# Group 1's weights split in the first pair of each attention, and the third pair reordered, in a hybrid attention and linear recurrence layer

## The chip, the cores and the metric

The kernel runs on one core of one Trainium2 chip. The metric is the device time of one execution in microseconds. A core has five engines with their own instruction streams: TensorE (PE), VectorE (DVE), ScalarE (ACT), GpSimd (POOL) and SyncE (SP), which here issues all DMAs. They wait for each other by semaphores. SBUF is the working memory, PSUM (eight banks) takes what PE writes.

## What is computed

One decoder layer on x of 2048 rows by 1024: RMS norm with shift and scale from a conditioning vector, one input projection to (attention q, k, v, gate; recurrence q, f, i, gate), a sliding-window attention with 16 query heads and 4 key heads of 64 columns, a gated linear recurrence with 8 heads of 128, and one output projection with gate and residual. All is float32. What bears on the change is the attention:

```
aq = rope(rms_norm(aq.reshape(B, S, 16, 64), q_norm_w), positions)
ak = rope(rms_norm(ak.reshape(B, S, 4, 64), k_norm_w), positions)
attn = sliding_window_attention(aq, ak, av, sinks) * silu(ag)
# blocks of 128 rows; each block of queries sees its own and the previous block of keys
s = q k^T * hd ** -0.5 ; s = where(mask, s, -inf)
m = max(max(s), sink) ; p = exp(s - m)
denom = sum(p) + exp(sink - m) ; o = (p / denom) v
```

## The kernel before

The 2048 rows are done as two segments of 1024 (s = 0, 1). For each segment there is a matrix product part (three units, `gemm_unit`), then the attention, then the recurrence. The output projection comes last. Each product is made of three single-pass products of split operands: a "hi" part (a copy rounded to the fast type, made by ACT) and a "lo" part (the rest, made by DVE as raw minus hi), so each weight has to be split before PE can use it.

**The attention** of a segment goes through 4 groups of heads with 8 blocks of 128 rows, 32 blocks b, taken in 16 pairs m (`att_pair`, one function for PE, one for ACT, one for DVE, each with an order written out by hand; POOL has `att_iter` for each block). In pair m PE projects the blocks 2m and 2m+1 (`project_block`, 24 matmuls of 384 columns each), turns q and k of the blocks j = 2m-2 and j+1 (`turn_qk`), turns the probabilities of the blocks p = 2m-4 and p+1 (`turn_p`), multiplies them with v (`values`) and makes new scores (`scores`) for the blocks j and j+1. So the third pair, m = 2, is the first with probabilities in it.

The path of a block b: PE projects it; ACT squares it (`squares_and_v`); DVE sums the squares (`sum_squares`); POOL makes the variance and the inverse root (L2739, L2741, `inverse_root`); DVE scales (`norm_qk`); POOL rotates q and k (L2779 to L2795; for block 0 DVE does q in `rotate_first`); PE turns them; ACT copies the hi (`turned_hi`), DVE the lo (`turned_lo`); PE makes scores; DVE masks them and takes the maxima (`mask_scores`); ACT exponentiates (`exps`); DVE inverts the sums (`invert_den`); ACT scales (`normalise`); PE turns (`turn_p`); ACT and DVE copy half of it each (`p_copy`). `project_block(b)` waits until block b-2 has been scaled, as both use one bank (`qkv_free`).

**The weights** of a group g (1536 KB) go to one buffer, `raw[0]`, and are split in 4 parts: `att_weights_hi` on ACT (semaphore `hi_ok`) and `att_weights_lo` on DVE (`lo_ok`). `next_weights(s, m)` on ACT and DVE says which parts of the next group are split in which pair. For group 1 in before: ACT makes parts 0 and 1 at the end of pair 1, 2 and 3 at the end of pair 2; DVE makes 0 and 1 in the middle of pair 2, 2 and 3 in the middle of pair 3. SP loads the next group once the last one has been split (`load_next`); group 1's load comes after the gate blocks of the attention, group 0's is asked for in the last unit of the products.

**Between products and attention** ACT, DVE, POOL and SP meet (`meet`, `phase_end`): none goes on until all five engines have arrived. SP arrives when all stores of the products have landed. PE arrives and goes on without waiting. Just ahead of it ACT makes the sines (`rotary_angles`) and DVE the rotary tables.

Of the kernel before, what the change touches and what calls it, by code (L numbers as in the profile page):

```python
# [29 lines left out]
QB = QUAD // P  # L30
# [46 lines left out]
def hybrid_layer(nc, x, xT, cT, pos, norm_w, w_ada, b_cols, b_gate, w_in, qk_w, sinks, rec_w, lbT, w_out,  # L77
                 ident_d, masks_d, causal_d, freq_d, out, mixed_T, nat, gate_T, x_T_d, root_d, a21_d, carry_k, carry_v):
    with ExitStack() as ctx:
# [421 lines left out]
        def _(sp):  # L501
# [60 lines left out]
            def gemm_unit(s, u):  # L562
# [33 lines left out]
                if not last:  # L596
                    sp.wait_ge(wlo_ok, PRODS * n + 7)
                    load_quarter(n + 1, B21)
                for c in range(4):
                    sp.wait_ge(comb_ok, comb(n, COMB_21, c))  # L600
                    block_out(s, u, u3[c], nat_u3, 1, 0, c)
# [21 lines left out]
            def attention(s):  # L623
# [40 lines left out]
                load_next(0)  # L664
# [228 lines left out]
        def _(pe):  # L893
# [335 lines left out]
            def att_pair(s, m):  # L1229

                j, p = 2 * m - 2, 2 * m - 4
                if 2 <= m <= PAIRS:
                    turn_qk(s, j)
                if m < PAIRS:
                    project_block(s, 2 * m, range(KH))
                    if m == 1:
                        turn_qk(s, j)
                    project_block(s, 2 * m, range(KH, KT))
                    project_block(s, 2 * m + 1, range(KH))
                    if m >= 1:  # L1240
                        turn_qk(s, j + 1)
                    project_block(s, 2 * m + 1, range(KH, KT - 2))
                    if m >= 2:
                        turn_p(s, p)
                    project_block(s, 2 * m + 1, range(KT - 2, KT))
                    if m >= 2:
                        turn_p(s, p + 1)
# [227 lines left out]
        def _(act):  # L1475
# [137 lines left out]
            def rotary_angles(s):  # L1613
                act.wait_ge(trig_step, s * 10 + 10)
                act.activation(sinv[:], ang[:], ACT.Sin).then_inc(trig_a, 1)
                act.activation(turns[:], ang[:], ACT.Abs).then_inc(trig_a, 1)
                act.wait_ge(trig_a, s * 3 + 2)
                act.activation(cosv[:], turns[:], ACT.Sin, bias=half_pi[:, 0:1], scale=-1.0).then_inc(trig_a, 1)

# [79 lines left out]
            def next_weights(s, m):  # L1699

                g, at = m // (NBLK // 2), m % (NBLK // 2)
                if g + 1 < GROUPS:
                    for part in (() if g == 0 else (0,), (0, 1) if g == 0 else (1,), (2, 3), ())[at]:
                        act.wait_ge(raw_in[0], 16 * w_use(s, 0, g + 1) + 16)
                        att_weights_hi(g + 1, part)
                elif at < 2:
                    rec_weights_hi(s, 0, (at,))

            def att_pair(s, m):

                j, p = 2 * m - 2, 2 * m - 4
                if 1 <= m <= PAIRS:
                    turned_hi(s, j)
                if 2 <= m <= PAIRS:
                    exps(s, p)
# [231 lines left out]
        def _(dve):  # L1947
# [412 lines left out]
            def next_weights(s, m):  # L2360

                g, at = m // (NBLK // 2), m % (NBLK // 2)
                if g + 1 < GROUPS:
                    for part in ((), () if g == 0 else (0,), (0, 1) if g == 0 else (1,), (2, 3))[at]:
                        att_weights_lo(s, g + 1, part)
                elif 1 <= at <= 2:
                    rec_weights_lo(s, 0, (at - 1,))

            def att_pair(s, m):

                j, p = 2 * m - 2, 2 * m - 4
                if 2 <= m <= PAIRS:
                    mask_scores(s, p)
                if 1 <= m <= PAIRS:
                    norm_qk(s, 2 * m - 1)
                if 2 <= m <= PAIRS + 1:
# [7 lines left out]
                if m < PAIRS:  # L2384
                    next_weights(s, m)
                if 2 <= m <= PAIRS + 1:
                    invert_den(s, p + 1)
                if m < PAIRS:
                    sum_squares(s, 2 * m)
                    norm_qk(s, 2 * m)  # L2390
# [7 lines left out]
                if 2 <= m <= PAIRS + 1:  # L2398
# [5 lines left out]
                if m < PAIRS:  # L2404
                    sum_squares(s, 2 * m + 1)
                if m == PAIRS:
# [518 lines left out]
```

## Time and profile before

| | |
|---|---|
| time, median of 3 runs | 1780.29 us (1779.18 to 1780.61) |
| profiled execution | 1780.95 us, span of its instructions 1779.1 us |
| PE busy | 1754.9 us, 9818 matmuls |
| DVE, ACT, POOL busy | 1276.8, 973.7, 480.9 us |
| granted TensorE clock | 1.000 over the span |
| first attention, from PE's first projection to the start of the recurrence | about 269.5 to 510 us |
| second attention | the same, 714.1 us later |

The page gives an engine's busy time; a wait is idle time of an engine, put down to the instruction that ended it. A timeline row reads: start in us, duration in us, engine, line of the kernel, operation, what it writes <- what it reads, shapes, how often in a row, and in brackets the idle time just before and who ended it. An instruction starts when it is issued to the engine's pipeline, so two of one engine may overlap a little.

### The profile page before, as it was taken

To read this page: it belongs to the slowest core of one execution; us is meant where nothing else is said; L and a number is where in the kernel's file an instruction comes from. 1 tells how busy PE (TensorE), PEld (TensorE's weight loads), DVE (VectorE), ACT (ScalarE), POOL (GpSimd) and SP (SyncE) were. 2 spreads that over 40 slices of the span, in tenths; PEclk is the share of its full clock that TensorE was granted. 3 is DMA by queue.
4 is the path that set the end of the run, shared out by engine and by line. 5 is a ranking of instruction groups with operands and counts; after the bars stand their busy time and mean duration, and the time that the engine had idled before them with its cause. 6 is when DMAs were issued, how large, how long until landed. Compare 5 with 4: busy or idle time off the path is not lost.

```text
span 1779.1 us, 28303 instructions
## 1 busy us (share of the span) xinstructions
PE 1754.9 (99%) x9818; PEld 1497.9 (84%) x9818; DVE 1276.8 (72%) x2610; ACT 973.7 (55%) x2127; POOL 480.9 (27%) x825
## 2 busy tenths in 40 slices
PE   7999999999999999999999999999999999999999
PEld 4888888999978888888888899997888888888887
DVE  7966466777766676796637677776776567987987
ACT  5622225888877665562222488887655565343441
POOL 1000026777722221210002677772221220000000
PEclk9999999999999999999999999999999999999999
DMA  9143232223124675334233322222433158178252
GB/s 371 67 171 108 100 109 99 76 72 87 41 99 107 173 182 156 125 130 166 98 116 106 105 76 76 65 60 69 152 101 98 51 179 316 63 250 303 109 178 95
DMA packets 168990, 227.03 MB, mean 128 GB/s; under 512 B 13072, under 2 KB 114832, under 8 KB 161168
## 3 DMA queue, kind: packets, MB, share of 16 engines
q1 hardware_dynamic: 168848, 225.22, 38.1%
q8 instruction: 79, 1.29, 0.3%
q14 instruction: 63, 0.52, 0.1%
HBM read 167.90 MB, written 57.28 MB: 127 GB/s over the span
## 4 chain that ended last, share of the span: by engine, by line
PE 87%; DVE 4%; issue 2%; DMA 2%; ACT 2%; POOL 2%; SPq 0%; POOLq 0%; ACTq 0%; DVEq 0%
PE bank L942 64%; PE bank L982 4%; PE bank L1225 3%; PE bank L1211 3%; PE bank L1195 3%; PE bank L1320 1%; PE bank L1300 1%; PE bank L1292 1%; PE bank L1335 1%; PE bank L1146 1%; DMA rg_w<-nat_rows 1%; PE bank L1325 1%; PE bank L929 1%; PE bank L1346 1%; DVE g_lo L2038 0%
## 5 line engine op out<-in xcount | busy, mean ns | idle before, releaser
L942 PE MATMUL bank<-h_hi,w_hi 128*128 128x512 f32 x512 | 206.3, 403 | 0.2
L942 PE MATMUL bank<-h_lo,w_hi 128*128 128x512 f32 x512 | 199.8, 390 | 0.0
L942 PE MATMUL bank<-h_hi,w_lo 128*128 128x512 f32 x512 | 199.7, 390 | 0.0
L942 PE MATMUL bank<-wq_hi,h_hi 128*128 128x384 f32 x512 | 179.6, 351 | 0.5 <-issue 0.5
L942 PE MATMUL bank<-ob_hi,oa_hi 128*128 128x512 f32 x448 | 175.1, 391 | 0.8 <-DVE ua L2534 0.5
L942 PE MATMUL bank<-ob_hi,oa_lo 128*128 128x512 f32 x448 | 174.4, 389 | 0.0
L942 PE MATMUL bank<-ob_lo,oa_hi 128*128 128x512 f32 x448 | 174.3, 389 | 0.0
L942 PE MATMUL bank<-wq_hi,h_lo 128*128 128x384 f32 x512 | 172.1, 336 | 0.0
L942 PE MATMUL bank<-wq_lo,h_hi 128*128 128x384 f32 x512 | 171.4, 335 | 0.0
L1514 ACT ACTIVATE g_hi<-g_raw 128x2048 fp32r<-128x2048 f32 x36 | 69.0, 1916 | 154.4 <-PE bank L942 127.8
L1664 ACT ACTIVATE sm<-sm,neg_m 128x257 f32<-128x257 f32 x256 | 127.6, 501 | 6.9 <-DVE neg_m L2301 1.8
L2038 DVE TENSOR_TENSOR g_lo<-g_raw,g_hi 128x2048 fp32r<-128x2048 f32 x35 | 80.6, 2303 | 57.4 <-ACT g_hi L1514 57.4
L942 PEld LDWEIGHTS bank<-h_lo,w_hi 128*128 128x128 f32 x512 | 96.1, 188 | 20.4
L942 PEld LDWEIGHTS bank<-h_hi,w_hi 128*128 128x128 f32 x512 | 96.3, 188 | 19.8 <-issue 1.6
L942 PEld LDWEIGHTS bank<-h_hi,w_lo 128*128 128x128 f32 x512 | 96.4, 188 | 18.2 <-issue 0.5
L2824 POOL TENSOR_TENSOR b_cum<-b_cum,mid_sum 128x256 f32<-128x256 f32 x32 | 20.9, 654 | 321.3 <-DVE mid_sum L2274 321.3
L1671 ACT ACTIVATE sm<-sm,r_den 128x256 f32<-128x256 f32 x256 | 105.8, 500 | 0.0
L942 PEld LDWEIGHTS bank<-ob_hi,oa_hi 128*128 128x128 f32 x448 | 84.1, 188 | 19.2 <-issue 2.0
L942 PEld LDWEIGHTS bank<-ob_hi,oa_lo 128*128 128x128 f32 x448 | 84.1, 188 | 17.6
L942 PEld LDWEIGHTS bank<-ob_lo,oa_hi 128*128 128x128 f32 x448 | 84.1, 188 | 17.1
L1789 ACT ACTIVATE oa_hi<-o_lower 128x1024 fp32r<-128x1024 f32 x40 | 42.5, 1062 | 100.7 <-PE bank L942 95.4
L942 PEld LDWEIGHTS bank<-wq_hi,h_hi 128*128 128x128 f32 x512 | 96.4, 188 | 1.3 <-issue 1.3
(268 smaller groups left out, 4653.3 us busy)
## 6 DMA issues: line engine op xcount, KB each, us to landing
g_raw<-in_w_in SPq DMA_DIRECT2D x24, 1024.0 KB, 7.5
raw<-in_w_in SPq DMA_DIRECT2D x16, 1024.0 KB, 9.1
o_lower<-mixed_cols SPq DMA_DIRECT2D x32, 512.0 KB, 6.8
nat_rows<-u SPq DMA_DIRECT2D x48, 256.0 KB, 2.9
raw<-in_w_in SPq DMA_DIRECT2D x8, 1536.0 KB, 6.8
o_upper<-in_w_out SPq DMA_DIRECT2D x24, 512.0 KB, 8.6
wa<-in_w_ada SPq DMA_DIRECT2D x8, 1024.0 KB, 11.5
g_q<-gate_cols SPq DMA_DIRECT2D x64, 128.0 KB, 2.8
```

The lines of the kernel that those rows point to most:

```text
L929: pe.matmul(bank[4 + i][:, :], c_bc[:, k - KH, :], wa[i][:, k, :], start=(k == MOD_PE[0][i]), stop=False)
L942: mm = pe.matmul(dst, a, b, start=(first and m == 0), stop=(last and m == 2), **more)
L982: mm = pe.matmul(ring(n, at + c)[:, :], operand(k)[h][:, tokens(c)], (g_hi, g_lo)[w][w_slot(n, e)][:, k, :], start=(first and k == 0), sto ...
L1195: mm = pe.matmul(score(j, h), tq[j % 2][lo:lo + HD, h // 2, :], tk[lo:lo + HD, k0:k0 + 2, :], start=(m == 0), stop=(m == 2))
L1211: mm = pe.transpose(bank[5 + h // 2][:, at:at + P], sm[j % 2][:, h, half * P:(half + 1) * P], ident[:])
L1225: mm = pe.matmul(dst[e * HD:(e + 1) * HD, :], vv[:, j % NBLK + half, :], pT[j % 2][:, e:GH:2, half, :], start=(half == 0), stop=(half == 1))
L1514: act.activation(g_hi[w_slot(n, e)][:], src[:], ACT.Copy).then_inc(whi_ok, 1)
L1664: act.activation(sm[j % 2][:, h, 0:2 * P + 1], sm[j % 2][:, h, 0:2 * P + 1], ACT.Exp, bias=neg_m[j % 2][:, h:h + 1], accum_out=den[j % 2][ ...
L1671: a = act.activation(sm[j % 2][:, h, 0:2 * P], sm[j % 2][:, h, 0:2 * P], ACT.Identity, scale=r_den[j % 2][:, h:h + 1])
L1789: act.activation(oa_hi[p][:], part_of(oa_raw[A_SLOT[e]], p), ACT.Copy).then_inc(oahi_ok, 1)
L2038: dve.tensor_tensor(g_lo[w_slot(n, e)][:], src[:], g_hi[w_slot(n, e)][:].bitcast(F32), ALU.subtract).then_inc(wlo_ok, 1)
L2824: pool.tensor_tensor(early, early, mid_sum[:].unsqueeze(2).to_broadcast([P, QB, CH]), ALU.subtract).then_inc(mid_ok, 1)
```

## The change

- SP asks for group 1's weights in the last unit of the products, behind the stores of the second block of columns and a wait for group 0's last low part; `load_next(0)` in the attention is gone.
- ACT makes group 1's hi parts 0 and 1 at the start of pair 0, behind the meeting; parts 2 and 3 stay at the end of pair 2.
- DVE makes group 1's lo parts 0 and 1 in pair 0, one behind each of the two sums of squares. In every pair that has two lo parts (3, 7, 11), the second moves behind the sum of squares.
- Third pair: PE turns block 2 in the middle of block 4 rather than ahead of it, and block 3 later in block 5; ACT does the exponentials of block 0 ahead of the copies of block 2; DVE masks block 1 ahead of scaling block 3, and copies the first probabilities ahead of scaling block 4.
- ACT does a small exponential of four columns behind the sines, at the end of `rotary_angles`.

```
@@ gemm_unit (SP), behind the stores of u2
                 if not last:
                     sp.wait_ge(wlo_ok, PRODS * n + 7)
                     load_quarter(n + 1, B21)
+                else:
+                    sp.wait_ge(lo_ok[0], w_parts(s, 0, 0, PARTS))
+                    load_att(1)
@@ attention (SP)
-                load_next(0)
                 load_rec(1)
@@ att_pair (PE)
-                if 2 <= m <= PAIRS:
+                if 3 <= m <= PAIRS:
                     turn_qk(s, j)
                 if m < PAIRS:
                     project_block(s, 2 * m, range(KH))
-                    if m == 1:
+                    if m in (1, 2):
                         turn_qk(s, j)
                     project_block(s, 2 * m, range(KH, KT))
                     project_block(s, 2 * m + 1, range(KH))
-                    if m >= 1:
+                    if m == 1 or m >= 3:
                         turn_qk(s, j + 1)
                     project_block(s, 2 * m + 1, range(KH, KT - 2))
+                    if m == 2:
+                        turn_qk(s, j + 1)
@@ rotary_angles (ACT)
+                act.activation(to_mid[0][:], half_pi[:, 0:QB], ACT.Exp)
@@ next_weights (ACT)
-                    for part in (() if g == 0 else (0,), (0, 1) if g == 0 else (1,), (2, 3), ())[at]:
+                    for part in (() if g == 0 else (0,), () if g == 0 else (1,), (2, 3), ())[at]:
@@ att_pair (ACT)
+                if m == 0:
+                    act.wait_ge(raw_in[0], 16 * w_use(s, 0, 1) + 16)
+                    for part in range(2):
+                        att_weights_hi(1, part)
+                if m == 2:
+                    exps(s, p)
                 if 1 <= m <= PAIRS:
                     turned_hi(s, j)
-                if 2 <= m <= PAIRS:
+                if 3 <= m <= PAIRS:
                     exps(s, p)
@@ next_weights (DVE)
-            def next_weights(s, m):
+            def next_weights(s, m, slot):
+                part = ((0, 1) if g == 0 else (None, None), (None if g == 0 else 0, None), (None if g == 0 else 1, None),
+                        (2, 3))[at][slot]
@@ att_pair (DVE)
                     mask_scores(s, p)
+                if m == 2:
+                    mask_scores(s, p + 1)
                 if 1 <= m <= PAIRS:
                     norm_qk(s, 2 * m - 1)
-                if 2 <= m <= PAIRS + 1:
+                if 3 <= m <= PAIRS + 1:
                     mask_scores(s, p + 1)
...
-                if m < PAIRS:
-                    next_weights(s, m)
+                if 0 < m < PAIRS:
+                    next_weights(s, m, 0)
                 if 2 <= m <= PAIRS + 1:
                     invert_den(s, p + 1)
                 if m < PAIRS:
                     sum_squares(s, 2 * m)
+                    next_weights(s, m, 0 if m == 0 else 1)
+                if m == 2:
+                    p_copy(s, p)
+                if m < PAIRS:
                     norm_qk(s, 2 * m)
...
-                if 2 <= m <= PAIRS + 1:
+                if 3 <= m <= PAIRS + 1:
                     p_copy(s, p)
...
                     sum_squares(s, 2 * m + 1)
+                if m == 0:
+                    next_weights(s, m, 1)
```

## Rows read from the trace of the kernel before

**Rows 1.** The page, busy time of PE, share of the span, instructions.
```profile
PE 1754.9 (99%) x9818; PEld 1497.9 (84%) x9818; DVE 1276.8 (72%) x2610; ACT 973.7 (55%) x2127; POOL 480.9 (27%) x825
```
**Rows 2.** Who PE waited for, whole span: us in total, times, longest.
```profile
PE bank L1146 <- POOL q_rot L2793: 2.1, 2, 1.0
...
PE bank L1211 <- ACT sm L1671: 0.8, 2, 0.4
```
**Rows 3.** Timeline of PE, first attention, pairs 1 and 2.
```profile
284.50 0.38 PE L1146 MATMUL bank<-ident,q_rot 128*128 128x128 f32 x2
...
289.86 0.44 PE L1146 MATMUL bank<-ident,q_rot 128*128 128x128 f32 x2 [1.03 <-POOL q_rot L2793]
...
298.64 1.09 PE L1211 MATMUL bank<-ident,sm 128*128 128x128 f32 x8 [0.40 <-ACT sm L1671]
```
**Rows 4.** Timeline of ACT, first attention, pairs 0 to 2.
```profile
274.02 0.44 ACT L1682 ACTIVATE sq<-bank 128x320 f32<-128x320 f32 x1 [9.99 <-PE bank L942]
...
278.10 0.44 ACT L1682 ACTIVATE sq<-bank 128x320 f32<-128x320 f32 x1 [3.53 <-PE bank L942]
...
287.68 1.58 ACT L1545 ACTIVATE wq_hi<-raw 128x768 fp32r<-128x768 f32 x2
...
290.64 0.39 ACT L1648 ACTIVATE qT_hi<-bank 128x256 fp32r<-128x256 f32 x1 [1.39 <-PE bank L1149]
...
291.21 1.28 ACT L1664 ACT_TABLE_LOAD   x1
...
296.89 3.30 ACT L1671 ACTIVATE sm<-sm,r_den 128x256 f32<-128x256 f32 x8
300.09 0.58 ACT L1696 ACTIVATE pT<-bank 128x512 f32<-128x512 f32 x1
```
**Rows 5.** Timeline of DVE, end of the products and first attention to pair 2.
```profile
261.21 3.56 DVE L2132 TENSOR_TENSOR wq_lo<-raw,wq_hi 128x768 fp32r<-128x768 f32 x4
...
274.49 0.49 DVE L2340 TENSOR_REDUCE q_ss<-sq 128x5 f32<-128x320 f32 x1 [0.91 <-ACT sq L1682]
...
280.75 0.49 DVE L2312 TENSOR_TENSOR qn<-bank,q_rinv 128x320 f32<-128x320 f32 x1 [1.66 <-POOL q_rinv L2741]
...
289.84 0.39 DVE L2301 SCALAR_TENSOR_TENSOR neg_m<-row_max,sink_neg 128x4 f32<-128x4 f32 x1
...
294.72 2.58 DVE L2132 TENSOR_TENSOR wq_lo<-raw,wq_hi 128x768 fp32r<-128x768 f32 x2
```
**Rows 6.** Timeline of SP's DMA issues, around the first meeting.
```profile
252.40 18.12 SPq L559 DMA_DIRECT2D nat_rows<-u  x8
272.78 1.93 SPq L628 DMA_DIRECT2D g_q<-gate_cols  x4
```
**Rows 7.** DMA issues of 236:237, 112:113 and 270:271: count, size, us to landing.
```profile
raw<-in_w_in SPq DMA_DIRECT2D x1, 1536.0 KB, 6.0
...
nat_rows<-u SPq DMA_DIRECT2D x2, 256.0 KB, 6.2
...
nat_rows<-u SPq DMA_DIRECT2D x1, 256.0 KB, 2.4
```
**Rows 8.** What SP's queue waited for, 240 to 330 us.
```profile
SPq L610 <- DMA nat_rows<-u: 1.9, 1, 1.9
```
**Rows 9.** Second attention: SP's first issue after the meeting, ACT's first squares.
```profile
987.54 0.33 SPq L648 DMA_DIRECT2D kT_hi<-carry_keys  x1
...
988.10 0.44 ACT L1682 ACTIVATE sq<-bank 128x320 f32<-128x320 f32 x1 [9.99 <-PE bank L942]
```
**Rows 10.** Timeline of POOL, first attention, pairs 0 to 2.
```profile
275.17 0.20 POOL L2739 TENSOR_SCALAR q_var<-q_ss 128x5 f32<-128x5 f32 x1 [31.87 <-DVE q_ss L2340]
275.45 1.20 POOL L2741 TENSOR_TENSOR q_rinv<-q_var,minus_half 128x5 f32<-128x5 f32 x1
...
284.24 0.46 POOL L2795 TENSOR_TENSOR k_rot<-rc,rs 128x128 f32<-128x128 f32 x1
...
295.30 1.19 POOL L2795 TENSOR_TENSOR k_rot<-rc,rs 128x128 f32<-128x128 f32 x1
```

More of the change, by code:

```diff
@@ L2358, in mix_block @@
                                          ALU.mult, ALU.mult).then_inc(omix_ok, 1)
-            def next_weights(s, m):
+            def next_weights(s, m, slot):
                 g, at = m // (NBLK // 2), m % (NBLK // 2)
+                part = ((0, 1) if g == 0 else (None, None), (None if g == 0 else 0, None), (None if g == 0 else 1, None),
+                        (2, 3))[at][slot]
                 if g + 1 < GROUPS:
-                    for part in ((), () if g == 0 else (0,), (0, 1) if g == 0 else (1,), (2, 3))[at]:
+                    if part is not None:
                         att_weights_lo(s, g + 1, part)
-                elif 1 <= at <= 2:
+                elif 1 <= at <= 2 and slot == 0:
                     rec_weights_lo(s, 0, (at - 1,))
```

## The prediction

> **What bounds the kernel now.** The page comes first: TensorE (PE) is busy for 99% of the span [rows 1]. So only two things can move the time: taking away one of PE's few waits, or making a new one. The list of who PE waited for, over the whole span, has only two entries that the attention can answer for: 2.1 us in two waits for POOL's rotated q, and 0.8 us in two waits for ScalarE's (ACT's) normalised probabilities [rows 2]. Each is two waits because there are two attentions. PE's timeline shows where they lie: both in the third pair (m = 2), 1.03 us before the turn of block 2 at 289.86 and 0.40 us before turn_p(0) at 298.64 [rows 3]. The second attention repeats this 714.1 us later. After the third pair PE has no wait in either attention. The whole prize is therefore about 3 us of 1780, 0.17%, and I ask as carefully what the edits put in front of PE in the first two pairs.
>
> **What the third pair gains.** (a) turn_qk(2) moves from ahead of block 4 to the middle of it, 12 matmuls later. PE waited 1.03 us [rows 3]; in that time it now does half of block 4's projection. A whole block takes 4.08 us, the distance of ACT's squares of blocks 0 and 1 at 274.02 and 278.10 [rows 4], half of it 2.04. The wait goes. (b) turn_p(0) waits for ACT. In before ACT copies q and k of block 2 (290.64 to 291.21), then loads a table for 1.28 us, and only then starts exps(0), at 292.49, though the row maxima were there at 290.23 [rows 4, 5]. Now the table is loaded right after rotary_angles, where ACT then sat idle for 9.99 us [rows 4]: cost nothing, and 1.28 us more if that cover were gone. exps(0) stands ahead of turned_hi(2) and can start 2.2 us sooner; the two copies (0.57 us) now lie between exps(0) and exps(1), so what follows comes 1.6 us earlier. mask_scores(1) fills DVE's wait for POOL's root, so exps(1) isn't held. normalise starts near 295.3 instead of 296.89, its first half (four of eight, 1.65 us) ends near 296.95. PE's own work from the turn of block 2 to turn_p(0) is 298.64 - 0.40 - 289.86 = 8.38 us, whatever its order; from 288.83, where its wait began, it comes to 297.21. The 0.40 us go too. Next in line is p_copy(0) on ACT, which lets turn_p(1) start: it ended at 300.67 (300.09 and 0.58) [rows 4] and now ends 1.6 us earlier, which is just in time for a PE that is 1.43 us earlier. With the restart after each wait I take **1.5 us for each attention, 3.0 in all**. The two DVE low parts (2.58 us) [rows 5] and the two ACT high parts that fed this pair are gone from here; they stand in pair 0 now.
>
> **What pair 0 pays on ACT and SP.** Group 1's weights are now asked for by SP as soon as group 0's last low part is done, at 261.21 + 3.56 = 264.77 [rows 5], in place of behind the gate blocks at 272.78 + 1.93 = 274.71 [rows 6]. Three things follow.
> First, the load goes ahead of the last four stores (256 KB each) of the last unit on SP's queue, the last of which SP issues at about 270.0 (half a us ahead of 252.40 + 18.12) and which lands 2.4 us later [rows 6, 7]. The phase meeting, at which ACT, DVE and POOL wait too, needs SP, and SP already waits 1.9 us for that store [rows 8]; the first work after it is at 272.78 [rows 6]. A load of 1536 KB alone lands in 6.0 us and 256 KB in 2.4 [rows 7], so by a straight line 1.7 us and 2.8 us for each 1024 KB. Load and four stores behind each other, 2560 KB, are then an estimated 8.9 us from 264.85: the last store lands at 273.75, not 272.4, and the meeting is some 1.1 us later (273.9). The bounds: nothing, if the stores go their own way, and 3.8 us, if the store takes 6.2 us, as two stores did that were issued just behind a load and a backlog [rows 7]. I take 1.1 us, nearer to the quiet rows, because SP's queue was idle before this load.
> Second, ACT makes two high parts of group 1 between the meeting and its first squares. Two took 1.58 us in before [rows 4]. They can't begin ahead of the meeting, and the weights have landed by then (alone at 264.85 + 6.0 = 270.85). The first squares started at 274.02 as PE's block 0 ended, 1.24 us behind the meeting [rows 4, 6]; now they start at 273.9 + 1.58 = 275.48, 1.46 us late. In the second attention the meeting was at 987.54 and the squares at 988.10 [rows 9], so they start at 988.64 + 1.58 = 990.22, 2.12 us late. With the meeting unmoved these would be 0.34 and 1.02.
> Third, load_rec(1) and the gate blocks follow the meeting as before; nobody waits for them in these pairs.
>
> **What pair 0 pays on DVE and POOL.** From the first squares to the turn of block 1 there is no slack. The sum of squares follows at 274.49, POOL's variance at 275.17 and its root at 275.45 [rows 5, 10]; DVE goes on with qn, the first rotation and the next sum, and waits 1.66 us for the next root before qn at 280.75 [rows 5]; POOL then rotates without a gap until k_rot(1) ends at 284.24 + 0.46 = 284.70, while PE stands at turn_qk(1) at 284.50 [rows 3, 10]. What is lost at the squares PE loses at this turn (part of it already where block 2 waits for qn of block 0), and the later links hang on PE itself.
> Into this chain the change sets a low part (0.89 us, a quarter of 3.56 [rows 5]) behind each of the two sums of squares, where DVE waits for POOL's root anyway. On DVE that costs nothing. But POOL's k_rot took 1.19 us instead of 0.46 just where DVE's low parts ran, at 295.30 [rows 5, 10]: POOL stood still until the first of them had ended. POOL's variance comes 0.19 us after the sum (274.98 and 275.17). If it is held until the low part ends, each root comes 0.89 - 0.19 us later, less some 0.04 by which DVE's instructions overlap: 0.66, twice, so 1.32 us for each attention. Bounds: nothing (the operand has only 5 columns; no row shows q_var beside a low part), and 0.89 us each time. I take 0.66, as the nearest row has the same DVE instruction.
> The Trainium skill speaks against this placement ("SBUF — State Buffer", Who interferes with whom): a DVE tensor_tensor with both inputs in SBUF shuts out a GpSimd instruction that reads SBUF until it has ended; the rule names no size. The k_rot row agrees. By that rule the cost is the 1.32 us, and without it nothing.
>
> **Other edits.** In pairs 3, 7 and 11 only the second low part moves, from ahead of invert_den(p+1) to behind the sum of squares. The sum comes 1.3 us earlier and the root, held 0.66 us, about 0.6 us earlier; PE has no wait there, so nothing. DVE's p_copy(0) now waits for turn_p(0) with norm_qk(4) queued behind it; block 6, the next to need that, comes a whole projected block later, so nothing, and some tenths of a us at turn_qk(4) if POOL's rotation of block 4 comes late. PE's own instructions are the same in number. I count nothing for TensorE's clock.
>
> **The sum.** Lost: 1.46 + 2.12 + 2 x 1.32 = 6.2 us. Gained: 3.0 us. Net +3.2 us. Against the profiled execution (1780.95, span 1779.1) that is 1784.15; the median of the runs shown is 0.66 us below it, 1780.29, so **1783.5 us**, 0.18% above.
>
> **The rivals.**
> A, the forecast: 1783.5, by its own bounds 1781.5 to 1785.5. Chance 0.50.
> B, POOL's small instructions are not held by a low part: 3.6 - 3.0 = +0.6, 1780.9. For it: only operands of 64 columns and more are seen held. Against: k_rot was held to the end. 0.12.
> C, the stores are not held back by the load: 0.34 + 1.02 + 2.64 - 3.0 = +1.0, 1781.3. For it: at 2.4 us each the stores leave the path idle for much of this stretch. Against: the 6.2 us row. 0.15.
> D, the faster side, B and C together: 1.36 - 3.0 = -1.6, 1778.7; the squares still come late, by ACT's two high parts. 0.10.
> E, clearly slower: the last store behind the load takes as long as the 6.2 us row, so it lands at 276.2, 2.45 us later than I take. Both attentions pay that: +4.9, 1788.4. It decides from the point where that store lands after 273.95; each further 0.1 us costs 0.2. 0.09.
> F, the change doesn't do what it says: p_copy and the new orders leave the waits of the third pair in another place, no gain: 1786.5. 0.04.
>
> **How the numbers follow.** 0.2% of this time is 3.56 us, about what a measurement of this kernel can tell from no change: slower starts at 1783.85, faster below 1776.7. The likeliest case lies just inside. Slower: two fifths of A (0.20), E and F, 0.33. Faster: D, if more is gained than I count, 0.02. Within: 0.65. The range from 1778.5 to 1786.5 takes in A, B, C, most of D and half of F, and leaves out E.
>
> **What would show it.** In the trace of after: SP's issue of group 1's load near 264.9 and the first instruction behind the meeting near 273.9 (A) or 272.8 (C); ACT's first squares at about 275.5 and 990.2; POOL's variance of block 0 at 0.9 us behind the sum (A) or 0.2 (B); PE waiting for q_rot or k_rot of block 1, or for qn of block 0, 2.8 us in all in the first attention and 3.4 in the second; no wait of PE at turn_qk(2), at most 0.3 us at turn_p(1); ACT's table load near 264. The prediction is wrong if PE's waits in pairs 1 and 2 together are under 1.5 us for each attention, or if PE waits again from pair 3 on.

## The result and the profile after

The changed kernel takes 1783.51 us, median of 18 runs (1780.23 to 1786.66); the kernel before takes 1779.65 (18 runs, 1778.01 to 1782.98). The ratio is 1.0020, 95% interval 1.0013 to 1.0026: 3.9 us slower. The forecast was 1783.5. The time agrees; the terms behind it agree only in part, and that is what the rest is about.

The profiled execution took 1783.37 us, span 1781.5. The page (against rows 1):
```profile
PE 1757.8 (99%) x9818; PEld 1502.2 (84%) x9818; DVE 1275.7 (72%) x2610; ACT 973.1 (55%) x2129; POOL 488.1 (27%) x825
```
PE has the same 9818 matmuls and is busy 2.9 us longer: some of them ran slower. Who PE waited for, whole span (against rows 2):
```profile
PE bank L944 <- DVE qn L2323: 5.0, 2, 3.1
```
The waits for q_rot (2.1 us) and for the probabilities (0.8 us) are gone. In their place PE waits 5.0 us, once in each attention, for the scaling of block 0: `project_block(2)` needs its bank. SP's issues, first and second attention (against rows 6 and 9):
```profile
264.89 0.34 SPq L506 DMA_DIRECT2D raw<-in_w_in  x1
265.49 5.12 SPq L559 DMA_DIRECT2D nat_rows<-u  x4
274.91 1.93 SPq L631 DMA_DIRECT2D g_q<-gate_cols  x4
...
990.19 0.33 SPq L651 DMA_DIRECT2D kT_hi<-carry_keys  x1
```
What SP's queue waited for, first attention (against rows 8), and the landings of issues at 264 to 265 us, 269.5 to 271 and 983 to 986 (against rows 7):
```profile
SPq L613 <- DMA nat_rows<-u: 4.0, 1, 4.0
...
raw<-in_w_in SPq DMA_DIRECT2D x1, 1536.0 KB, 7.1
...
nat_rows<-u SPq DMA_DIRECT2D x1, 256.0 KB, 4.6
...
nat_rows<-u SPq DMA_DIRECT2D x1, 256.0 KB, 5.7
```
The load is asked for where the prediction said, and the last store lands 4.6 and 5.7 us after its issue, against 2.4 and 3.3 in before. The first work behind the meeting is at 274.91 and 990.19. ACT's timeline (against rows 4):
```profile
264.15 1.28 ACT L1623 ACT_TABLE_LOAD   x1
...
274.87 1.58 ACT L1549 ACTIVATE wq_hi<-raw 128x768 fp32r<-128x768 f32 x2 [9.22 <-SPq L355]
276.35 0.42 ACT L1687 ACTIVATE sq<-bank 128x320 f32<-128x320 f32 x1
...
293.76 0.51 ACT L1669 ACTIVATE sm<-sm,neg_m 128x257 f32<-128x257 f32 x1 [2.21 <-DVE neg_m L2312]
...
991.63 0.42 ACT L1687 ACTIVATE sq<-bank 128x320 f32<-128x320 f32 x1
```
The squares of block 0 come at 276.35 and 991.63 (274.02 and 988.10 before). The table load is out of the way. POOL's timeline (against rows 10):
```profile
277.47 0.74 POOL L2760 TENSOR_SCALAR q_var<-q_ss 128x5 f32<-128x5 f32 x1 [34.08 <-DVE q_ss L2351]
...
282.09 0.77 POOL L2760 TENSOR_SCALAR q_var<-q_ss 128x5 f32<-128x5 f32 x1 [0.24 <-issue]
...
286.98 0.73 POOL L2814 TENSOR_TENSOR q_rot<-rc,rs 128x256 f32<-128x256 f32 x1
```
The variance takes 0.74 and 0.77 us instead of 0.20. PE's timeline (against rows 3), both waits and some of the matmuls behind them:
```profile
280.08 0.45 PE L944 MATMUL bank<-wq_hi,h_hi 128*128 128x384 f32 x1 [1.92 <-DVE qn L2323]
...
280.90 0.33 PE L944 MATMUL bank<-wq_lo,h_hi 128*128 128x384 f32 x1
281.07 0.34 PE L944 MATMUL bank<-wq_hi,h_lo 128*128 128x384 f32 x1
...
282.03 0.52 PE L944 MATMUL bank<-wq_hi,h_hi 128*128 128x384 f32 x1
282.35 0.52 PE L944 MATMUL bank<-wq_lo,h_hi 128*128 128x384 f32 x1
...
288.39 0.38 PE L1148 MATMUL bank<-ident,q_rot 128*128 128x128 f32 x2
...
995.45 0.69 PE L944 MATMUL bank<-wq_hi,h_hi 128*128 128x384 f32 x1 [3.11 <-DVE qn L2323]
...
1001.38 0.46 PE L944 MATMUL bank<-wq_lo,h_hi 128*128 128x384 f32 x1
1001.68 0.34 PE L944 MATMUL bank<-wq_hi,h_lo 128*128 128x384 f32 x1
```
A matmul that follows the last by 0.17 us follows it by 0.32 from 281.42 to 284.59, and from 995.45 to 1001.4. The busy times by stretch say why. A row has the stretch, its length, the busy time (and number of instructions) of PE, PEld, DVE, ACT and POOL, then the granted clock, the DMA share and GB/s:
```profile
264.90:269.90 5.00, 4.74 (x22) 3.69 (x21) 2.38 (x4) 0.74 (x2) 0.00 (x0) 1.00 0.85 261
269.90:274.90 5.00, 5.00 (x31) 5.00 (x30) 2.85 (x9) 0.03 (x1) 0.00 (x0) 1.00 0.77 264
...
282.00:285.00 3.00, 3.00 (x12) 2.90 (x12) 1.63 (x4) 0.55 (x2) 2.23 (x3) 0.53 0.02 5
285.00:290.00 5.00, 5.00 (x32) 4.97 (x31) 0.97 (x3) 1.10 (x4) 4.51 (x10) 1.00 0.01 3
...
995.00:1000.00 5.00, 4.55 (x16) 4.46 (x16) 3.57 (x8) 0.00 (x0) 3.53 (x6) 0.50 0.51 198
```
After the wait TensorE was at its lower level, 1.2 GHz, for 3.2 and some 6 us, and then at 2.4 GHz again.

**How late each attention makes PE.** I compare the start of the same turns in two profiled executions, less the difference already there ahead of the attention. For the changed kernel: turn_qk(1) is 3.79 us late in the first attention and 6.22 in the second; by the turn of block 6 it is 1.81 and 4.46, at the end 1.26 and 3.91, together 5.2. The medians differ by 3.9. The profiled execution of before was 1.3 us above its median, and every other kernel's trace, faster or slower, is 0.8 to 1.7 us shorter than it in the recurrence between the attentions, which none of them changes; I take this as variation between executions, not as something that the change gives back: the kernel of experiment 3 is within 0.02 us of before in the first attention and 1.0 us shorter in the recurrence behind it. Outside the two attentions together the traces differ from the one of before by -2.8 us (the changed kernel, 2.4 us longer as a whole) to +0.5, so only the attentions and the medians are compared here. The ledger of all kernels, in us, with the median beside the one of before measured along with it:

| kernel | attention 1 | attention 2 | sum | medians |
|---|---|---|---|---|
| changed kernel | +1.26 | +3.91 | +5.2 | +3.9 |
| load asked for early | +1.15 | +2.04 | +3.2 | +2.8 |
| and ACT's high parts | +2.35 | +3.30 | +5.7 | +5.7 |
| and DVE's low parts (all splits) | +3.36 | +4.50 | +7.9 | +7.8 |
| load asked for behind the last store | +0.02 | +0.04 | +0.1 | +0.7 |
| changed, low parts late | +1.39 | +3.34 | +4.7 | +3.6 |
| changed, PE's wait filled | +0.95 | +1.20 | +2.2 | +2.8 |
| orders alone | -1.03 | -1.41 | -2.4 | -2.8 |
| orders, both low parts behind the sum | -1.53 | -1.88 | -3.4 | -3.8 |
| the same, load behind the last store | -1.57 | -1.87 | -3.4 | -3.2 |
| orders, low parts in the fourth pair | -0.72 | -0.76 | -1.5 | -1.7 |
| second low part alone | -0.79 | -0.81 | -1.6 | -2.2 |

### The profile page after: what moved, and what is told of

The parts are those of the page before. It is cut to its first block, busy times and chain, and to the rows that moved or that the text cites. A ratio compares the mean times of both kernels' runs of the same rounds, so it can differ in the third digit from the quotient of the medians.

```text
span 1781.5 us, 28305 instructions
## 1 busy us (share of the span) xinstructions
PE 1757.8 (99%) x9818; PEld 1502.2 (84%) x9818; DVE 1275.7 (72%) x2610; ACT 973.1 (55%) x2129; POOL 488.1 (27%) x825
## 4 chain that ended last, share of the span: by engine, by line
PE 91%; DVE 4%; DMA 2%; ACT 1%; issue 1%; POOL 0%; SPq 0%; POOLq 0%; ACTq 0%; DVEq 0%
PE bank L944 67%; PE bank L984 4%; PE bank L1227 3%; PE bank L1213 3%; PE bank L1197 3%; PE bank L1296 2%; PE bank L1324 2%; PE bank L1339 2%; PE bank L1304 2%; PE bank L1148 1%; PE bank L1350 1%; PE bank L1329 1%; PE bank L931 1%; DMA nat_rows<-u 1%; DVE g_lo L2049 0%
## 5 line engine op out<-in xcount | busy, mean ns | idle before, releaser
L944 PEld LDWEIGHTS bank<-wq_lo,h_hi 128*128 128x128 f32 x512 | 97.8, 191 | 0.0
```

The costliest lines, as they stand in the source:

```text
L944: mm = pe.matmul(dst, a, b, start=(first and m == 0), stop=(last and m == 2), **more)
```

## Experiments

**1. The two halves.** The orders alone: the changed kernel with the load, the high parts and the low parts back where they were.
```
-                else:
-                    sp.wait_ge(lo_ok[0], w_parts(s, 0, 0, PARTS))
-                    load_att(1)
...
+                load_next(0)
                 load_rec(1)
```


> The third pair's new order on all engines and the early table load, with group 1's load and splits where the kernel before has them (ACT at the end of pairs 1 and 2, DVE's parts 0 and 1 in pair 2, the second behind the sum of squares). Theory of the prediction: the meeting and the squares of block 0 stay at 272.8 and 274.0, PE loses its 1.03 and 0.40 us waits, and each attention ends 1.5 us earlier: about 1776.7 (3.0 us under before). Rival 1, the order gives nothing because ACT's copy of the probabilities takes the place of the waits: 1779.7. Rival 2, it is gained and given back in the recurrence: the attention ends 1.5 us earlier in the trace, but the end of the program doesn't.

Measured 1777.07 us, ratio 0.9986 (0.9977 to 0.9995). The splits alone are the kernel before with the other half:

> The kernel before with only the early load of group 1 and its parts 0 and 1 split in pair 0 (ACT behind the meeting, DVE behind the two sums of squares); third pair and table load as before. Theory: all losses of the change and none of its gains. The meeting comes at 274.9 and 990.1, PE stands before block 2 for 1.9 and 3.1 us, and each attention is some 3.5 and 5.2 us later, 1788 in all. Rival, the losses come from the new order and not from the splits: about as before, 1779.7.

Measured 1787.62, ratio 1.0050 (1.0036 to 1.0064), in 5 runs, and PE stands before block 2 for 1.97 and 3.15 us, as expected. So the change is a gain of 2.8 us and a loss of 7.8. Their sum is 5.0 and not 3.9, but the intervals are wide enough for that, and in the traces (the table above) it is 5.5 against 5.2. The gain is 1.03 and 1.41 us for the attentions, not the 1.5 expected, and PE's wait for q_rot hasn't gone. What the orders alone leave, PE, POOL and DVE in pair 2:
```profile
298.55 0.44 PE L1146 MATMUL bank<-ident,q_rot 128*128 128x128 f32 x2 [0.88 <-POOL q_rot L2807]
```
```profile
294.77 1.60 POOL L2796 TENSOR_TENSOR rs<-qn,rot 128x128 f32<-128x128 f32 x2
...
296.62 1.20 POOL L2801 TENSOR_TENSOR rs<-qn,rot 128x32 f32<-128x32 f32 x2
```
```profile
294.53 1.10 DVE L2137 TENSOR_TENSOR wq_lo<-raw,wq_hi 128x768 fp32r<-128x768 f32 x1
...
296.54 0.95 DVE L2137 TENSOR_TENSOR wq_lo<-raw,wq_hi 128x768 fp32r<-128x768 f32 x1
```
The wait moved from turn_qk(2) to turn_qk(3): the low parts hold POOL's rotation (1.60 and 1.20 us here; 0.88 and 0.46 for the same instructions of block 1 at 285.43 and 286.56 of the changed kernel, with no low part beside them).

**2. The load alone, then with the high parts.** The load alone is before with one edit: `load_att(1)` ahead of the last stores, `load_next(0)` gone.

> The kernel before with one edit: group 1's raw weights are asked for ahead of the carry's stores (about 265 us of the profile, 979 us in the second attention) instead of behind the meeting; all splits, orders and ScalarE's table stay as they were. Theory (the meeting is on the path): SP's first work behind the meeting comes at about 274.9 and 990.2 us, as in the changed kernel, so the squares of block 0 start 0.9 us late in the first attention and 2.0 us late in the second (the changed kernel's +2.33 and +3.53, less the 1.5 us of ScalarE's two splits there), SP's wait for the carry's stores grows from 1.9 and 2.7 to about 4 and 5 us, and all that follows is late by the same: some 2.9 us, a median near 1782.5. Rival (the squares have slack to TensorE's turns): the squares late by as much, but turn_qk(1) late by less than half of it, 1780 to 1781. Second rival (the store does not wait behind the load, and the later meeting of the changed kernel came of its splits): no change at the meeting, 1779.7.

Measured 1782.69, ratio 1.0017 (1.0008 to 1.0025). With ACT's two high parts in pair 0:
```
+                if m == 0:
+                    act.wait_ge(raw_in[0], 16 * w_use(s, 0, 1) + 16)
+                    for part in range(2):
+                        att_weights_hi(1, part)
```


> The load alone, and with it ScalarE's two high splits of group 1 in pair 0, behind the meeting and ahead of the squares, as in the changed kernel; VectorE's low parts stay in pairs 2 and 3 of the group, and the third pair keeps its old orders. Theory: the squares of block 0 start 1.5 us later again than with the load alone (one split at 1.58 us, the other in idle time in front of it), POOL's q_var stays at 0.20 us since no low part of VectorE lies beside it, and so the median is 1.5 times 2 = 3.0 us above the load alone, less what the third pair gets back where ScalarE no longer splits there ahead of turned_hi (turn_qk(2)'s wait of about 1 us in each attention): 1783.5, between 1782 and 1785.5. The step from here to the kernel with all splits (1787.6) is then the price of VectorE's low parts beside POOL's first chain: 1.3 us an attention by q_var's two holds, and TensorE's clock. Rival (the splits fill idle time of ScalarE, and only VectorE's low parts cost): within 0.5 us of the load alone.

Measured 1785.62, ratio 1.0032 (1.0019 to 1.0044), in 5 runs. The squares' part of this was right. But the wait at turn_qk(2), of which about 1 us was to be given back, is still 1.02 us in the first attention (0.36 in the second), and the median lies just above the range. The first squares of both attentions, ACT's timeline, of the load alone:
```profile
275.09 0.44 ACT L1684 ACTIVATE sq<-bank 128x320 f32<-128x320 f32 x1 [11.02 <-SPq L355]
...
989.66 0.44 ACT L1684 ACTIVATE sq<-bank 128x320 f32<-128x320 f32 x1 [12.01 <-SPq L355]
```
and with the high parts, with POOL's first variance:
```profile
276.47 0.41 ACT L1684 ACTIVATE sq<-bank 128x320 f32<-128x320 f32 x1
```
```profile
277.58 0.20 POOL L2745 TENSOR_SCALAR q_var<-q_ss 128x5 f32<-128x5 f32 x1 [34.23 <-DVE q_ss L2346]
```
Each step is in the time: 2.8 us for the load (the meeting), 2.9 for the high parts, 2.1 from here to all splits, which is the low parts beside POOL. In the traces this last step is 1.0 and 1.2 us. In the first attention the clock falls in neither of the two kernels, so there the 1.0 us is the low parts alone. The variance takes 0.20 us without them and 0.74 with them. The Trainium skill's rule ("SBUF — State Buffer", Who interferes with whom), that a DVE tensor_tensor with both inputs in SBUF shuts out a GpSimd instruction reading SBUF, agrees: it holds for an operand of 5 columns too.

**3. The load behind the stores.** The load alone, asked for after the last store instead of ahead of the last four.
```
                 for c in range(4):
                     sp.wait_ge(comb_ok, comb(n, COMB_21, c))
                     block_out(s, u, u3[c], nat_u3, 1, 0, c)
+                if last:
+                    sp.wait_ge(lo_ok[0], w_parts(s, 0, 0, PARTS))
+                    load_att(1)
```


> The load alone again, but asked for just behind the last of the carry's stores instead of ahead of them; it is still ahead of the meeting. Theory (the early load costs because the stores that the meeting waits for land behind its 1536 KB): SP's wait for the stores and its first work behind the meeting are those of the kernel before (1.9 and 2.7 us; 272.8 and 987.5), the squares come at 274.0 and 988.1, and the median is that of the kernel before, 1779.5 to 1780.3. Rival (any load in flight at the meeting holds up the landing of the last store, issued 2 us before, in whichever order they are asked for): the meeting is late by 1 to 2 us in each attention, 1781.5 to 1782.7, as with the load ahead.

Measured 1781.33, ratio 1.0004 (0.9996 to 1.0013), which is a gain of 0.7 to a loss of 2.3 us; the median lies between what the theory (to 1780.3) and the rival (from 1781.5) give, and decides nothing. The trace is plain. Landings of the issues at 269.5 to 271.5, and ACT's first squares:
```profile
raw<-in_w_in SPq DMA_DIRECT2D x1, 1536.0 KB, 7.7
nat_rows<-u SPq DMA_DIRECT2D x1, 256.0 KB, 2.9
```
```profile
274.00 0.44 ACT L1684 ACTIVATE sq<-bank 128x320 f32<-128x320 f32 x1 [9.99 <-PE bank L944]
```
The store lands after 2.9 us with the load right behind it (4.6 with the load in front), SP waits 1.6 us for it (1.0 in the second attention), and every turn of both attentions is within 0.05 us of before. So the late meeting comes from the load being ahead of the stores, not from a load being in flight at the meeting. Not shown is whether the place in the queue does it or only the earlier time: no run asks for the load as early on another queue. The Trainium skill ("DMA: Bandwidth & Descriptors", Queues, rings and completion order) says that each DMA engine takes the descriptors of a queue in order, which fits these landings.

**4. Low parts late.** The changed kernel, its low parts back in pair 2.
```
-                part = ((0, 1) if g == 0 else (None, None), (None if g == 0 else 0, None), (None if g == 0 else 1, None),
-                        (2, 3))[at][slot]
+                part = ((None, None), (None if g == 0 else 0, None), (0, 1) if g == 0 else (1, None), (2, 3))[at][slot]
```


> The changed kernel, but DVE makes group 1's lo parts 0 and 1 in pair 2 rather than behind the two sums of squares of pair 0. Theory (a lo part holds POOL's variance back by 0.66 us, twice for each attention): POOL's variance takes 0.20 us again in place of 0.74, PE's wait before block 2 falls by about 0.6 us in each attention, and the time by 2.6 us or a little more, to about 1780.7. Rival, POOL isn't on the path because PE is held by the squares alone: no change, 1783.5.

Measured 1783.44, ratio 1.0024 (1.0016 to 1.0033): no gain, a miss. PE's wait before block 2 falls by 0.3 and 0.2 us only (1.62 and 2.92), not by 0.6. At turn_qk(1) PE is 2.31 and 4.79 us late, some 1.5 us less than in the changed kernel, but in pair 2 the same low parts hold POOL again, PE waits 0.87 and 0.72 us at turn_qk(3), and by the turn of block 4 the first attention has nothing left of it (1.72 us late, 1.61 in the changed kernel), the second 0.8. A low part costs where it lies beside POOL's chain, in whichever pair.

**5. PE's wait filled.** In the changed kernel PE does 12 (first segment) and 18 (second) matmuls into a bank whose content nobody uses, ahead of `project_block(2)`, so that it isn't idle there.
```
+                if m == 1:
+                    for _ in range(12 + 6 * s):
+                        pe.matmul(bank[7][:, 0:QKV], h_hi[:, 0, tokens(2)], region(wq_hi[0], QKV)[:, 0, :], start=True,
+                                  stop=True)
```


> The changed kernel with extra matmuls of 384 columns on PE between blocks 1 and 2 (12 in the first attention, 18 in the second; their result goes to a bank nobody reads), so that PE does not stand idle for 1.9 and 3.1 us. Theory of the clock (the granted clock fell to its lower level because PE stood idle): it stays at the upper level, matmuls of the pair stay at 0.17 us apart, and PE is 0.25 and 1.5 us earlier at the turn of block 1: about 1781.8. Rival, the fall has another cause and PE's own work sets it: the slow matmuls stay and the time is as for the changed kernel or above it, 1783.5.

Measured 1782.59, ratio 1.0014 (1.0005 to 1.0023). The median lies between the theory's 1781.8 and the rival's 1783.5; the trace decides. The granted clock stays at 2.4 GHz, and in the first attention PE waits at the turn instead:
```profile
282.00:285.00 3.00, 3.00 (x19) 2.82 (x18) 1.46 (x5) 1.10 (x4) 2.31 (x4) 1.00 0.01 3
...
995.00:1000.00 5.00, 5.00 (x31) 4.97 (x30) 2.89 (x7) 0.87 (x3) 4.00 (x8) 1.00 0.33 133
```
```profile
287.24 0.44 PE L1148 MATMUL bank<-ident,q_rot 128*128 128x128 f32 x2 [0.65 <-POOL q_rot L2818]
```
From the first squares to turn_qk(1) it takes 11.38 us in the first attention and 11.48 in the second (275.86 to 287.24, 990.37 to 1001.85), the changed kernel 12.04 and 13.35 (276.35 to 288.39, 991.63 to 1004.98). The 0.66 and 1.87 are what the lower clock cost there: in the changed kernel q_rot was done at 287.71 and PE came 0.68 later. The second attention of the filled kernel is 2.7 us better in the ledger, and 0.9 of that isn't the clock: the last store landed after 4.8 us here, and after 5.7 to 6.1 us in the five other traces with the load ahead of the stores.

In the medians filling gains 0.9 us only, with intervals that overlap. How low the clock was in the other executions can be told from the mean granted clock of each, known to three digits. Of the changed kernel's 18 executions one has 1.000, ten have 0.999, four 0.998 and three 0.997, the profiled one among these. Of the filled kernel's 11 ten have 1.000, and of the 27 of before measured along with it 24. So nearly every execution of the changed kernel loses clock, most of them less than the profiled one. Its seven executions at 0.997 and 0.998 have a median of 1785.1 us, the other eleven one of 1782.7.

**6. Where the low parts should lie.** The orders alone, with low parts 0 and 1 both behind the sum of squares of pair 2:
```
+                parts = (((), ()), ((), ()) if g == 0 else ((0,), ()), ((), (0, 1)) if g == 0 else ((1,), ()), ((2,), (3,)))[at][slot]
```


> The orders alone, with group 1's low parts 0 and 1 both behind the sum of squares of the third pair, where the orders alone had one ahead of it and one behind it. Theory (what is left of the wait at turn_qk(3), 0.88 and 0.54 us with the orders alone, is the low part that VectorE puts ahead of the sum of squares, and by it ahead of POOL's chain): POOL's q_ss arrives 0.95 us sooner, the wait at turn_qk(3) falls to 0.3 us or less in both attentions, the median is 0.5 to 1.2 us below that of the orders alone: about 1776.2. Rival (two low parts in a row behind the sum hold POOL's chain by its shared port just as long): the same wait as with the orders alone, or a longer one, 1777 to 1778.

Measured 1776.15, ratio 0.9975 (0.9966 to 0.9984). POOL and PE in pair 2:
```profile
296.34 1.17 POOL L2809 TENSOR_TENSOR k_rot<-rc,rs 128x128 f32<-128x128 f32 x1
```
```profile
297.57 0.33 PE L1149 MATMUL bank<-ident,k_rot 128*128 128x128 f32 x1 [0.36 <-POOL k_rot L2809]
```
Of the rotation only k_rot is held now (and the variance behind it, 0.79 us), and 0.36 us of the 0.88 are left (nothing listed in the second attention). With all four low parts in the fourth pair:

> The orders alone, with no low part of group 1 in the third pair: parts 0 and 1 go to the fourth pair, ahead of its sum of squares, and 2 and 3 behind the sum. Theory (the low parts are what delays POOL in the third pair, and the fourth has room for them): no wait of TensorE at turn_qk(2) or turn_qk(3), each attention 1.0 to 1.6 us shorter than with the orders alone, a median of about 1774.8. Rival (the fourth pair has no room: four low parts of 0.95 us there delay norm_qk and p_copy, and by them turn_p): the wait moves to the fourth pair or to the projection of group 1's first block, which needs all four parts, and the median is that of the orders alone or above it, 1777 to 1779.

Measured 1778.24, ratio 0.9992 (0.9983 to 1.0001): the rival was right. By the turn of block 4 this kernel has gained 1.77 and 1.74 us, more than any other, and the third pair has no wait. Then DVE and PE in the fourth pair:
```profile
307.12 2.54 DVE L2137 TENSOR_TENSOR wq_lo<-raw,wq_hi 128x768 fp32r<-128x768 f32 x2
...
310.04 1.81 DVE L2137 TENSOR_TENSOR wq_lo<-raw,wq_hi 128x768 fp32r<-128x768 f32 x2
...
313.33 0.68 DVE L2353 COPY pT<-bank 128x512 f32<-128x512 f32 x1
```
```profile
314.16 1.06 PE L1211 MATMUL bank<-ident,sm 128*128 128x128 f32 x8 [1.68 <-DVE pT L2353]
```
p_copy queues behind the norm, the norm behind low parts, and 1.6 us go back.

**7. The second low part alone.** Before, with only this, in pairs 3, 7 and 11:
```
                     sum_squares(s, 2 * m)
+                    next_weights(s, m, 1)
                     norm_qk(s, 2 * m)
```


> The kernel before with one edit: in the fourth, eighth and twelfth pair (groups 0, 1 and 2) VectorE's last low part stands behind the sum of squares instead of ahead of it. Everything else is as before. In the prediction this edit counted for nothing. Theory now (from the turns of TensorE in the traces: in pairs 7 and 11 the second transpose of scores comes 2.20 us behind the first in the kernel before and 1.94 us in every kernel that has this edit, because the copy of the first transposes no longer queues behind a late norm of q and k): 0.27 us less in each of pairs 7 and 11 of both attentions, 1.1 us in all, a median near 1778.6. Rival (it really is worth nothing, and the later TensorE turns only shift): within 0.3 us of the kernel before.

Measured 1778.42, ratio 0.9990 (0.9981 to 0.9999). In the trace each of the three pairs gives 0.27 us, pair 3 as well, 1.6 in all. The two turns of probabilities in pair 7, PE's timeline of before (not among the rows ahead) and of this kernel:
```profile
370.51 1.03 PE L1211 MATMUL bank<-ident,sm 128*128 128x128 f32 x8
372.71 1.06 PE L1211 MATMUL bank<-ident,sm 128*128 128x128 f32 x8
```
```profile
370.92 1.03 PE L1211 MATMUL bank<-ident,sm 128*128 128x128 f32 x8
...
372.86 1.04 PE L1211 MATMUL bank<-ident,sm 128*128 128x128 f32 x8
```
2.20 us apart, and 1.94. In before DVE's p_copy ends at 372.56, just ahead of the second turn:
```profile
371.88 0.68 DVE L2348 COPY pT<-bank 128x512 f32<-128x512 f32 x1
```
It queues behind the norm and so behind both low parts. From this I read a wait of PE of 0.27 us; the profile puts none in brackets for it.

**8. A kernel faster than both.** The kernel of experiment 6 beats both. With the load behind the last store added to it:

> The orders alone with both low parts of the third pair behind its sum of squares (1776.2), and group 1's load asked for just behind the carry's last store. Theory: the raw weights then land 3 us sooner, but in this order no split waits for them, so nothing is gained: within 0.6 us of 1776.2. Rival (the load in flight delays the last store, and so the meeting, by 1 to 2 us an attention): 1778 to 1779.5.

Measured 1777.47, ratio 0.9980 (0.9971 to 0.9989). That is 0.7 us above the upper end of what was expected, but 3.2 us under before as measured along with it, where experiment 6 has 3.8. The trace gives -1.57 and -1.87 us, as without it (-1.53 and -1.88). In the traces an earlier load is worth nothing where no split waits for it.

## Why the prediction came out right, and where it was wrong

**What pair 0 pays on ACT and SP: mechanism right, size wrong.** I took the last store to land at 273.75 and the meeting 1.1 us late; it was 2.0 and 2.5 us late (274.91 and 990.19, less 0.10 and 0.19 that the executions differed already). The mis-sized term is the straight line through two quiet rows [rows 7], which gave 2560 KB in 8.9 us. The rows of stretches show 261 and 264 GB/s for 10 us from the load's issue on, which is those 2560 KB (2.62 MB) in 10.0 us. Choosing "nearer to the quiet rows" was the error: load and stores mixed don't move at the rate of a load alone. By single microseconds the load alone moved 406 to 442 GB/s (238.5 to 241.5 of before), load and stores together 209 to 382 (265.9 to 273.9). There is a slip in the sum, too: by its own figures the store lands 1.35 us later (273.75 against 272.4), not 1.1, and a meeting that follows the store by 0.38 us as in before would be at 274.1. In the second attention the last store took 5.7 us, but with 3.3 in before it was later there already. The squares came 2.23 and 3.34 us late, against 1.46 and 2.12. Rival E's condition, the store landing after 273.95, was met (about 274.6), at less than half the price that it named, and C is out: of the two experiments with the load alone, the one ahead of the stores costs 2.8 us, the one behind them nothing in the trace. D, which needs B and C together, is out with it.

**What pair 0 pays on DVE and POOL: right, slightly large.** The hold was taken as 0.66 us by k_rot's row; q_var's rows say 0.74 and 0.77 where 0.20 stood, so 0.54 and 0.57, 1.11 us for each attention and not 1.32. Rival B is out. "No slack" between squares and turn was not quite true: in the filled kernel the squares are 2.19 and 2.43 us late, with the holds that makes 3.30 and 3.54, and turn_qk(1) is 3.09 and 3.44 late, so 0.2 and 0.1 us were slack.

**"I count nothing for TensorE's clock": the step that failed.** The prediction said itself that part of the loss would be a wait for the scaling of block 0, and expected 2.8 and 3.4 us of wait up to the turn of block 1. It did not ask what PE does after such a wait. PE waited 1.92 and 3.11 us, more than the 1.5 that the prediction had set as the least, and then at 1.2 GHz it lost 0.66 and 1.87 us more on the way to turn_qk(1). So PE is late there by 3.79 and 6.22 us, not 2.78 and 3.44.

**What the third pair gains: right, slightly small.** From turn_qk(1) to the turn of block 6 the changed kernel wins back 1.98 and 1.76 us where I took 1.5. No wait at turn_qk(2), none at turn_p(1), the table load at 264.15, as said. exps(0) starts at 293.76 straight behind its maxima. So rival F is out. What I had not seen is that this rests on the low parts being gone from pair 2: with them there the same orders win 0.5 and 0.9 us only.

**Other edits: wrong.** The second low part "gains nothing" because "PE has no wait there". I read that off the list of waits. The turns are 0.27 us late in each of these pairs [the two rows of experiment 7], and pairs 7 and 11 give it back in both attentions, 1.1 us. In pair 3, where the edit alone gives 0.27 us too, the changed kernel loses 0.2 us in the first attention and nothing in the second; there the two turns of probabilities are still 2.21 us apart (314.33 and 316.54), with p_copy ending at 316.39, so the short wait is still in place. The other 0.2 us of the first attention I didn't follow.

**The sum.** Predicted 1.28 and 1.92 us for the attentions, measured 1.26 and 3.91 in the trace. Against the prediction, first attention: squares +0.77, holds -0.21, slack -0.2, clock +0.66, the stretch from turn_qk(1) to block 6 -0.48, pairs 7 and 11 -0.55, and these cancel. Second: +1.22, -0.21, -0.1, +1.87, -0.26, -0.55, which is +2.0. The trace therefore says 5.2 us and the medians 3.9. That the time hit 1783.5 is in part luck: a balance of errors of 0.2 to 2 us, and a typical execution that loses less than the profiled one. The granted clocks of experiment 5 say where that may come from. The mean shortfall from 1.000 of the 18 executions is 0.0015, half of the profiled one's 0.003, so the clock costs a typical one an estimated half of the 2.5 us (0.66 and 1.87), 1.3 us less. That would be the whole difference between 5.2 and 3.9, but three digits are coarse, and only one execution of the changed kernel has a trace, so it is an estimate and not shown.

## What to carry to other kernels

A load put early into a queue is paid by the stores behind it, and dearly when a meeting waits for the last of them (2.8 us here): ask for it behind the last store, if no one needs it sooner. When an edit moves a wait of TensorE ahead of a long run of matmuls, price those at the lower clock too, from rows at both levels, not only the wait. And look for waits in the distances of like turns, since the list of waits leaves out what is short: here it hid 1.6 us.

## What the runs showed of the hardware

- **The clock after a wait.** PE was at the full level ahead of every one of these waits and busy. After waits of 1.92, 2.49, 2.92, 3.11 and 3.15 us the granted clock fell to 0.50 for some microseconds; after waits of 1.25, 1.53, 1.62, 1.64, 1.68 and 1.97 us it did not. After 2.49 and 3.11 us the first matmul was slow already, after 1.92, 2.92 and 3.15 seven or eight ran at full speed first. The splits alone, first attention, no fall after the longer wait of the two that are nearly equal:
```profile
281.32 0.44 PE L944 MATMUL bank<-wq_hi,h_hi 128*128 128x384 f32 x1 [1.97 <-DVE qn L2318]
...
282.00:285.00 3.00, 3.00 (x20) 2.97 (x19) 2.00 (x5) 0.55 (x2) 2.61 (x5) 1.00 0.09 36
```
  against 1.92 us and 0.53 in the changed kernel. From these rows no rule for when it falls can be had.
- **A small operand is held as well.** A DVE low part (both inputs in SBUF) holds even a POOL instruction on 5 columns to its own end: 0.20 us become 0.74 to 0.79.
- **Queue order.** A 256 KB store lands in 2.9 and 3.1 us with 1536 KB right behind it, and in 4.6 to 6.1 us with 1536 KB and three stores ahead of it (twelve landings, six traces).
